# A hybrid attention and state-space layer on one core: readout products on four 64x64 tiles, and GpSimd's residual multiply behind the attention

## The reference, cut to what matters

```python
xn = rmsnorm(h, norm1_g)
q, k, v, u, gates = split(xn @ w_in)
attn = stick_breaking_attention(rmsnorm(q), rmsnorm(k), v)
y = s5_ssm(u, ...)                  # Re(C x) + D u, x a complex diagonal recurrence
g = gelu(y); ssm = g * sigmoid(g @ w_glu + b_glu)
mixed = sigmoid(gate_a) * (attn @ w_attn_proj) + sigmoid(gate_s) * (ssm @ w_ssm_proj)
h = h + mixed @ w_o
h = h + (silu(conv_g) * conv_v) @ w_down   # conv over rmsnorm(h) @ w_up
```

## Time and profile before

| | us |
|---|---|
| median of three runs | 713.1 (712.81 to 713.95) |
| the profiled execution | 712.44 |
| its span in the trace | 710.7 |
| PE busy | 702.5 |
| DVE busy | 415.4 |
| ACT busy | 319.7 |
| POOL busy | 187.6 |

### The profile page before, as it was taken

One profiled execution on the slowest core, in us unless ns is written; L12 is line 12 of the kernel. 1 busy time (PEld: TensorE's weight loads), 2 busy tenths in 40 slices (PEclk: granted clock), 3 DMA queues, 4 the chain that ended last, 5 costly groups with the idle time before them and its releaser, 6 DMA issues.

```text
span 710.7 us, 13993 instructions
## 1 busy us (share of the span) xinstructions
PE 702.5 (99%) x5552; PEld 668.8 (94%) x5552; DVE 415.4 (58%) x557; ACT 319.7 (45%) x474; POOL 187.6 (26%) x215
## 2 busy tenths in 40 slices
PE   8999999999999999999999999999999999999998
PEld 7899899989999999999999999999999998888887
DVE  5764488867787756545765666666666662222221
ACT  4754343558888654435443444443343442211220
POOL 7899999940000022232011010101011010000000
PEclk9999999999999999999999999999999999999999
DMA  8163444545211233333333332323333343333331
GB/s 230 56 201 81 95 126 97 106 96 164 60 33 60 66 90 112 89 90 92 89 99 100 95 89 89 89 89 89 89 98 97 105 121 89 97 96 96 96 97 45
DMA packets 140520, 69.25 MB, mean 97 GB/s; under 512 B 24067, under 2 KB 138471, under 8 KB 140479
## 3 DMA queue, kind: packets, MB, share of 16 engines
q1 hardware_dynamic: 140319, 68.65, 35.0%
q10 hardware_dynamic: 160, 0.02, 0.0%
HBM read 63.19 MB, written 4.28 MB: 95 GB/s over the span
## 4 chain that ended last, share of the span: by engine, by line
PE 90%; DVE 3%; ACT 3%; SPq 1%; issue 1%; DMA 1%; POOL 0%; DVEq 0%; ACTq 0%
PE ps L1803 81%; PE ps L1987 1%; PE ps L2045 1%; PE ps L1854 1%; PE ps L1952 1%; PE ps L2012 1%; ACT xh L982 1%; SPq L626 1%; DMA xtok<-in_x_dram 1%; SPq L533 1%; ACT hi L913 1%; PE ps L1863 1%; PE ps L1921 1%; PE ps L1904 0%; PE ps L1947 0%
## 5 line engine op out<-in xcount | busy, mean ns | idle before, releaser
L1296 DVE TENSOR_TENSOR lo<-raw,hi 128x1024 fp32r<-128x1024 f32 (+2 forms) x102 | 136.5, 1339 | 152.6 <-ACT hi L913 152.3
L1803 PE MATMUL ps<-xh,hi 128*128 128x264 f32 (+1 forms) x1088 | 219.6, 283 | 0.1
L1803 PE MATMUL ps<-xl,hi 128*128 128x264 f32 (+1 forms) x1088 | 218.7, 282 | 0.0
L913 ACT ACTIVATE hi<-raw 128x1024 fp32r<-128x1024 f32 (+2 forms) x102 | 111.5, 1093 | 237.1 <-PE ps L1803 232.3
L1803 PE MATMUL ps<-xh,lo 128*128 128x264 f32 (+1 forms) x1088 | 217.9, 282 | 0.0
L1803 PEld LDWEIGHTS ps<-xh,hi 128*128 128x128 f32 x1088 | 167.2, 189 | 1.7 <-issue 0.8
L1803 PEld LDWEIGHTS ps<-xl,hi 128*128 128x128 f32 x1088 | 166.7, 188 | 0.0
L1803 PEld LDWEIGHTS ps<-xh,lo 128*128 128x128 f32 x1088 | 166.7, 188 | 0.0
L896 POOL TENSOR_TENSOR cv<-cv 128x512 f32<-128x512 f32 x22 | 28.4, 1289 | 226.7 <-DVE cv L1755 226.7
L1803 PE MATMUL ps<-ah,hi 128*128 128x512 f32 (+1 forms) x198 | 74.3, 375 | 0.0
L1803 PE MATMUL ps<-al,hi 128*128 128x512 f32 (+1 forms) x198 | 73.1, 369 | 0.0
(11 more groups left out here) (291 smaller groups left out, 966.1 us busy)
## 6 DMA issues: line engine op xcount, KB each, us to landing
raw<-in_w_up_dram SPq DMA_DIRECT2D x88, 256.0 KB, 3.1
raw<-in_w_in_dram SPq DMA_DIRECT2D x52, 256.0 KB, 3.4
raw<-in_w_down_dram SPq DMA_DIRECT2D x16, 384.0 KB, 3.3
raw<-in_w_down_dram SPq DMA_DIRECT2D x16, 320.0 KB, 4.0
raw<-in_w_o_dram SPq DMA_DIRECT2D x16, 256.0 KB, 2.9
xtok<-in_x_dram SPq DMA_DIRECT2D x4, 512.0 KB, 5.7
raw<-in_w_ssm_proj_dram SPq DMA_DIRECT2D x8, 256.0 KB, 2.9
out_dram<-yt SPq DMA_DIRECT2D x7, 256.0 KB, 2.4
```

What stands on the lines that cost most here:

```text
L913: act.activation(hi[slot][:, 0:n * P], raw[slot][:, 0:n * P], ACT.Copy)\
L1296: dve.tensor_tensor(lo[slot][:, 0:n * P], raw[slot][:, 0:n * P], hi[slot][:, 0:n * P].bitcast(F32), ALU.subtract)\
L1803: ins = pe.matmul(o, weights[w], acts(a, c), start=start and i == 0, stop=stop and i == 2)
```

## The change

POOL waits for `av_ps` to reach 4 (the last head's `values` products are done) before it multiplies the residual. And each carried-state product of `readout` is issued as two products with 64 rows by 64 columns of weights, one for the lower and one for the upper half of the output partitions: 64 instead of 32 in each of four rounds.

```diff
@@ POOL
             pool.wait_ge(rb_in, 16)
+            pool.wait_ge(av_ps, HEADS)
             for k in range(KD):
                 pool.tensor_tensor(hT[:, k, :], hT[:, k, :], rb[:], ALU.mult).then_inc(h_raw, 1)
@@ PE, readout(r)
                 for c in range(2):
                     for g in range(2 * RP):
                         part = slice(ST * (g % 2), ST * (g % 2) + ST)
-                        ins = pe.matmul(group_out(g), hout[r % HOUTS][part, c, g // 2, 1:T8 + 1, :]
-                                        .rearrange("p i h -> p (i h)"),
-                                        xst[part, c, g // 2, :], start=False, stop=c == 1,
-                                        skip_group_check=True)
+                        maps = hout[r % HOUTS][part, c, g // 2, 1:T8 + 1, :]\
+                            .rearrange("p i h -> p (i h)")
+                        for half in range(2):
+                            mine = slice(ST * half, ST * half + ST)
+                            ins = pe.matmul(group_out(g)[mine], maps[:, mine],
+                                            xst[part, c, g // 2, :], start=False, stop=c == 1,
+                                            skip_group_check=True)
                 ins.then_inc(y_ps, 1)
```

## The result

The changed kernel takes 721.2 us (median of four runs, 720.17 to 723.93) against 712.98 before: ratio 1.0119, 95% interval 1.0104 to 1.0134. It is slower, as forecast, but by 8.2 us where 4.2 were forecast. The profiled execution took 721.74 us, its span 720.0. Lines behind the change have moved by one (POOL) or four (PE).

A forecast was written before the change was run, and what follows sets the result against it. PE was taken to bound the kernel, busy 99% of the span. 712.44 - 1.5 (four tiles) + 5.65 (moved multiplies) = 716.6 us profiled; with 0.66 for the median, 717.3 us, range 715.2 to 719.5.

The forecast's parts named there:

- Line 1952 on four tiles: In each SSM round's readout, 64 products on four tiles take 1.09 us instead of 1.93, saving 0.84 us.
- The instruction bound: Rival, 15%: 34 ns per product is a floor, so each readout loses 0.25 us; 719.3 us in all.
- What arrives of it: Of the four readout savings, -1.5 us arrives by suffix(0): 0.65 by prep(3) and beyond, plus round 2's 0.84.
- the 0.65 from rounds 0 and 1: At prep(3), 0.5 us earlier, plus 0.15 of PE's wait for ACT's copy, whose chain moves by round 0's 0.84.
- waits away: What readout(3) saves beyond 1.49 us is lost waiting before scores and suffix, behind SP and ACT; worth nothing.
- What the move removes: About 0.9 us of waiting in DVE's line 1516 before readout(3) goes, but is worth nothing at the end.
- part 1: The carried-state products on four tiles in the SSM rounds: -1.5 us in all, or +0.5 with +0.25 a round.
- What the move adds: Behind the attention, POOL's multiplies make DVE 6.5 us late; space_part(0) starts 5.65 us later, none given back.
- six blocks: Six of POOL's eight multiplies, 1.19 us each, stand in DVE's way behind the attention.
- my rule of alternation: DVE and POOL operations with two SBUF operands hold each other off entirely and so take turns.
- The clock: Rival, 4%: PE's 2.4 and 3.2 us waits halve the clock for the next output tile, 4.3 us; 721.6 us.
- The range: 715.2 to 719.5 us: from four blocks with the full saving up to the instruction bound with some margin.

The follow-up runs named there:

- fed: Changed kernel plus unread PE products during its waits (20 before scores(0), 16 before attention_part(0), 22 before space_part(0)): 719.02 us, ratio 1.0077 to the kernel before.
- move_only: Kernel before with only POOL's added wait for av_ps, carried-state products as before: 719.48 us, ratio 1.0099.
- one_operand: Changed kernel with POOL's eight multiplies by a constant instead of rb, residual not rescaled: 714.8 us, ratio 1.0034 to the kernel before.
- half_moved: Changed kernel with four of POOL's eight multiplies at once beside the SSM rounds, four behind the attention: 717.29 us, ratio 1.0058 to the kernel before.
- four_and_one: both_heads with four multiplies once sl of all tiles is set, one behind line 883's first sum, none behind the second: 711.85 us, ratio 0.9982 to kernel before.
- head_first: Changed kernel with ACT making head 0's k and qh before gelu(3), POOL's multiplies one by one behind its sums: 719.58 us, ratio 1.0106 to kernel before.
- both_heads: spread with head 1's k and qh also ahead of gelu(3): 712.26 us, ratio 0.9988 to the kernel before.
- spread: head_first_old with three multiplies at once, three when sl of all tiles is set, one behind each of two sums: 712.64 us, ratio 1.0004 to kernel before.
- tiles_only: Changed kernel without the added av_ps wait, so the four 64x64 tiles alone: 713.01 us, ratio 1.0004 to the kernel before.
- head_first_old: head_first with POOL's multiplies in their old place beside the SSM rounds: 713.97 us, ratio 1.0016 to the kernel before.
- phase: Changed kernel with PE's 20 idle products at the start cut into 80 of 32 columns each: 751.8 us.

## Why the prediction was wrong

- **Line 1952 on four tiles.** Right: 1.09 us a round. The instruction bound (15%) falls; 17 ns a product is also below the floor of 25 ns of the Trainium skill's page that I weighed, which the trace contradicts for products on different tiles: four of them start 6 to 7 ns apart, and the next four some 58 ns behind.
- **What arrives of it.** Wrong, the first step that failed: -1.5 forecast, +0.9 measured. Up to readout(2) it looks nearly right, 1.15 us earlier instead of 1.49 (prep(3) at 132.59 rather than 132.4, released by DVE and not by POOL, and line 1970 at 135.64, 0.32 earlier rather than 0.65). But 0.34 of it is the head start at readout(0), so it is luck: round 2's own 0.84 arrived, and of the 0.65 from rounds 0 and 1 nothing. (From readout(0) to toep(3), the other kernels with four tiles, fed left aside, gain 0.7 to 1.4 us.) The chain from round 0 could not move by 0.84, since SP was not free:

```profile
100.80 5.09 SPq L670 DMA_DIRECT2D gates<-norm_dram  x8
106.00 5.18 SPq L626 DMA_DIRECT2D uc<-u_dram  x8
```

Line 626 started right behind line 670's eight DMAs and so only 0.45 earlier than in the earlier trace rows, with the head start in it. Then I moved SP's row of issues as a block. Between toep(3)'s first issue and y_write(2)'s last end lie 12.4 us, 10.9 before: 1.5 of the gain are gone there, with 0.34 from above and some 0.15 at the landing that makes the 2.0 us between forecast (158.07 - 1.49) and measurement at gelu(3). What PE "waits away" before scores(0) I priced at nothing; behind that wait of 2.65 us the clock halves, which costs 1.4 us of a unit. suffix(0) came at 171.9 instead of 169.0.
- **What the move removes.** Right: worth nothing at the end. Lines 1516 and 1517 take 0.43 us each, readout(3) starts 2.1 us earlier (1.15 of it by part 1), and PE waits this away before scores(0). move_only shows the same without the four tiles. The waiting in line 1516 was 1.13 us and not 0.9.
- **What the move adds.** Right in size, 6.5 us late, six blocks, +5.6, and in mechanism for the larger part. one_operand shows the second operand as the cause of about two thirds of it; the rest came with one operand too, for which my rule of alternation has no place. half_moved shows how DVE's spare time counts: with four multiplies DVE was 2.3 us late, and PE waited 1.3.
- **The clock.** Wrong. I had two waits of 2.4 and 3.2 us in the sum and gave their effect on the clock 4%, because no row before had such a wait. Behind most such waits here it fell: that cost 2.8 us behind space_part(0) in the profiled execution, and 2.2 us between the medians with and without feeding. The rival's price of 4.3 us was too high by its sum (one whole output tile) and its 721.6 came out near the measured 721.2 only because the clock fell at two places and part 1 brought no gain.
- **The range.** Its upper end took the instruction bound in and left the clock out. move_only's 719.5 would have been at its edge.

## What to carry to other kernels

Where PE is 99% busy, a wait of about 2 us can cost more than itself: forecast every new wait with its length, and if it is as long as those behind which the clock fell here (1.6 us and more), add the products behind it at half speed for 3.4 us or more, as a rival with a high chance; behind two such waits here the clock stayed up. Ahead of a move of a GpSimd operation with two SBUF operands, look for the moments when DVE is idle while nothing of its own kind is due, not for a stretch where DVE is idle on average; and spread the operations over those moments (four_and_one). A saving on PE is only worth what the next chain over SP and ACT lets through; here it took a new order on ACT and a new place for the multiplies to release it, and 1.5 us in all. And compare two profiled executions from the last point where they should be equal, not from zero.

## What the runs showed of the hardware

**The lower clock.** In the profiled executions, PE's waits up to 1.3 us (before, one_operand, head_first, both_heads, four_and_one) never had a halved clock behind them. Waits of 1.6 us (spread), 2.1 (half_moved), 2.2 (tiles_only, head_first_old), 2.65 (changed) had, and it lasted 3.4 to 6.8 us; the pairs 2.2 and 1.9 (changed) and 2.2 and 2.9 (move_only) 10.2 and 3.4 us. phase repeats the changed kernel's: 2.55 us with 3.4, the pair 2.2 and 1.8 with 10.2. It isn't certain: in fed a wait of 2.7 us before prep(3) passed with the clock up, and so did move_only's first, of 2.2. This may also be what widens the runs: the changed kernel's four lie 3.8 us apart, with mean granted clocks of 0.988 to 0.995, and some of the slower executions of the kernel before have lower ones too (714.99 us at 0.994).

**Instruction transfers and SP.** The DMA view of 144.8 to 146.4 and of 153.8 to 155.9 us in the changed kernel (queue and kind: packets, MB, share) has one transfer of instructions in each, at the two long issues of SP. The first of the two:

```profile
q8 instruction: 1, 0.02, 3.6%
```

It is one packet of 16 KB (0.02 MB). Between 100 and 160 us every issue of SP above 0.7 us overlaps such a packet in time, in the kernel before (108.9, 121.6, 129.6 and 155.2 us) as in the changed one (106.5, 117.5, 126.5, 137.7, 145.1 and 154.0). Before, one packet came at 144.0, while SP was waiting for readout(2), and cost nothing. All profiled kernels with the four tiles have a packet right behind readout(2), when SP issues toep(3); the two without have it before. The other twelve profiled kernels show the same coincidence without exception. And the length of SP's row from toep(3) to the last y_write(2) goes with where the next packet falls: in tiles_only and head_first_old it meets the weight loads behind that row, which takes 11.3 and 10.8 us; in the other ten with four tiles it meets a y_write, and the row takes 12.0 to 12.8. The Trainium skill ("Runtime: NRT & Kernel Launch", section "Instruction fetch mechanics") says that each engine refills its instructions in blocks of 16 KiB or 256 instructions: the change adds 64 of PE's instructions a round (32 products, 32 loads), 256 in all, and the page of the profile counts 30 packets instead of 29, which fits. That the packet causes the long issue, and that the added instructions moved it there, is what the coincidences say and was not shown; phase added 240 instructions, nearly one whole block, and so could hardly shift the packets.

**Short float32 products.** In the idle products at the start, the trace of phase has 32 columns streamed at 0.215 us each, the changed kernel's 128 columns took 0.154 in the mean:

```profile
1.07 31.14 PE L1835 MATMUL ps<-ones 128*128 128x32 f32 x145 [1.07 <-POOL ones L721]
```

```profile
1.07 6.16 PE L1831 MATMUL ps<-ones 128*128 128x128 f32 x40 [1.07 <-POOL ones L721]
```

The eight idle products that follow have 128 columns in both kernels. Phase:

```profile
35.81 3.78 PE L1831 MATMUL ps<-ones 128*128 128x128 f32 x16
```

The changed kernel:

```profile
8.46 2.05 PE L1831 MATMUL ps<-ones 128*128 128x128 f32 x16
```

So it is the clock. In the changed kernel the first dozen products start 0.213 us apart and the later ones 0.112, and the trace's first record of the upper level is at 4.1 us. In phase all 160 start 0.213 apart, and that record comes only at 51.6 us (ahead of the first record the views print 1.00, which says nothing). At the lower level 32 columns took as long as 128. There were four times as many products, and PE stayed at the lower level behind them: that is where the 33 us come from. That the short products kept the clock down fits, but no other run tests it.
